# One unread 128-column product per pass of the gate and up loops, and no drain before them

## The reference, cut to what matters

```python
def swiglu(h, w_gate, w_up, w_down):
    return (jax.nn.silu(h @ w_gate) * (h @ w_up)) @ w_down
```

## Time and profile before

| | |
|---|---|
| median of 3 executions | 1468.01 us (1467.56 to 1468.77) |
| profiled execution: its time, its span | 1475.34 us, 1473.5 us |
| PE busy | 1450.0 us, 98% of the span |
| DVE busy | 1000.9 us, 68% |
| ACT busy | 808.7 us, 55% |
| mean granted share of TensorE's clock | 0.996 |
| first loop (layer `f0`), second loop (layer `f1`) | from 82.48 us to 253.95 us, from 600.25 us to 778.43 us |

### The profile page before, as it was taken

One profiled execution on the slowest core, in us unless ns is written; L12 is line 12 of the kernel. 1 busy time (PEld: TensorE's weight loads), 2 busy tenths in 40 slices (PEclk: granted clock), 3 DMA queues, 4 the chain that ended last, 5 costly groups with the idle time before them and its releaser, 6 DMA issues.

```text
span 1473.5 us, 23721 instructions
## 1 busy us (share of the span) xinstructions
PE 1450.0 (98%) x8739; PEld 1260.8 (86%) x8739; DVE 1000.9 (68%) x1447; ACT 808.7 (55%) x1240; POOL 128.4 (9%) x77
## 2 busy tenths in 40 slices
PE   9999999999999999999999999999999899999997
PEld 9999999888986789999998888888678788888875
DVE  7499998433684345888984336335784799898885
ACT  6456666222555434566663325443882478887774
POOL 0520000000000005200000000000110012222111
PEclk9999999999999999999999999999999999999999
DMA  6223333322320213223333232322007499999994
GB/s 258 87 86 114 103 100 113 133 93 101 115 86 1 72 61 112 72 99 114 114 105 124 86 117 70 132 86 86 30 1 285 181 357 395 392 392 393 382 374 121
DMA packets 36216, 226.28 MB, mean 154 GB/s; under 512 B 5271, under 2 KB 5527, under 8 KB 11824
## 3 DMA queue, kind: packets, MB, share of 16 engines
q1 hardware_dynamic: 31248, 211.53, 38.3%
q0 software_dynamic: 4608, 13.22, 3.9%
q10 hardware_dynamic: 288, 0.55, 0.1%
HBM read 215.22 MB, written 13.63 MB: 155 GB/s over the span
## 4 chain that ended last, share of the span: by engine, by line
PE 55%; DMA 5%; DVE 2%; ACT 2%; issue 1%; POOLq 0%; ACTq 0%; DVEq 0%; SPq 0%
PE PS L275 16%; PE PS L277 16%; PE PS L276 16%; DMA eraw<-experts 4%; PE PS L2089 1%; PE PS L2109 1%; PE PS L2100 1%; PE PS L2851 1%; PE PS L1863 0%; DVE WEL L2985 0%; PE PS L2487 0%; ACT WEH L2922 0%; PE PS L316 0%; DMA out<-X,expert_index 0%; PE PS L2874 0%
## 5 line engine op out<-in xcount | busy, mean ns | idle before, releaser
L270 DVE TENSOR_TENSOR WL<-raw,WH 128x2048 fp32r<-128x2048 f32 x53 | 124.5, 2349 | 217.3 <-ACT WH L265 217.2
L2985 DVE TENSOR_TENSOR WEL<-eraw,WEH 128x2048 fp32r<-128x2048 f32 x96 | 217.6, 2286 | 21.2 <-ACT WEH L2922 20.9
L265 ACT ACTIVATE WH<-raw 128x2048 fp32r<-128x2048 f32 x51 | 97.7, 1916 | 221.4 <-PE PS L277 221.4
L2922 ACT ACTIVATE WEH<-eraw 128x2048 fp32r<-128x2048 f32 x96 | 182.2, 1914 | 33.9 <-DMA eraw<-experts 23.4
L275 PE MATMUL PS<-AH,WL 128*128 128x256 f32 (+1 forms) x624 | 181.5, 291 | 2.1 <-DVE WL L270 0.9
L276 PE MATMUL PS<-AL,WH 128*128 128x256 f32 (+1 forms) x624 | 180.7, 290 | 0.0
L277 PE MATMUL PS<-AH,WH 128*128 128x256 f32 (+1 forms) x624 | 180.7, 290 | 0.0
L275 PE MATMUL PS<-WH,AL 128*128 128x512 f32 (+2 forms) x416 | 155.0, 372 | 0.6 <-DVE AL L2321 0.3
L277 PE MATMUL PS<-WH,AH 128*128 128x512 f32 (+2 forms) x416 | 152.5, 367 | 0.0
L276 PE MATMUL PS<-WL,AH 128*128 128x512 f32 (+2 forms) x416 | 152.5, 367 | 0.0
L275 PEld LDWEIGHTS PS<-AH,WL 128*128 128x128 f32 x624 | 118.1, 189 | 5.8 <-DVE WL L270 1.3
(11 more groups left out here) (395 smaller groups left out, 3503.5 us busy)
## 6 DMA issues: line engine op xcount, KB each, us to landing
eraw<-experts SPq DMA_DIRECT2D x96, 1024.0 KB, 16.1
raw<-stream SPq DMA_DIRECT2D x94, 1024.0 KB, 4.9
out<-X SPq DMA_DIRECT2D x5, 512.0 KB, 7.0
moe_rows<-moe_rows_g SPq DMA_DIRECT2D x5, 512.0 KB, 6.5
X<-x SPq DMA_DIRECT2D x4, 512.0 KB, 6.0
ffn_row<-rows SPq DMA_DIRECT2D x2, 512.0 KB, 10.3
final_row<-rows SPq DMA_DIRECT2D x2, 512.0 KB, 6.9
cst<-consts SPq DMA_DIRECT2D x1, 739.5 KB, 15.3
```

Of the source, the lines that this page charges most:

```text
L265: act.activation(unit_home(WH, u, at), raw[:, u % SLOTS, :], ACT.Copy).then_inc(unit_hi, 1)
L270: dve.tensor_tensor(unit_home(WL, u, at), raw[:, u % SLOTS, :], unit_home(WH, u, at).bitcast(F32), ALU.subtract).then_inc(unit_lo, 1)
L2922: act.activation(WEH[:, k % ESLOTS, :], eraw[:, k % ERAW, :], ACT.Copy).then_inc(unit_hi, 1)
L2985: dve.tensor_tensor(WEL[:, k % ESLOTS, :], eraw[:, k % ERAW, :], WEH[:, k % ESLOTS, :].bitcast(F32), ALU.subtract).then_inc(unit_lo, 1)
```

## The change

Each pass of the loop gets one product of 128 columns. It multiplies a block of the low part of the tokens by itself and writes columns 256 to 384 of bank 7, which nothing reads. It stands ahead of the even unit, behind the two waits of its first quarter. The wait of line 797 is taken out.

```diff
+                def shake(bank, n):
+                    for _ in range(n):
+                        pe.matmul(PS[:, bank, 256:384], AL[:, 3, 0:P], AL[:, 3, 0:P], start=True, stop=True)
+
...
                 pe.wait_ge(silu_made, 4)
-                pe.wait_ge(unit_used, u0 + 4)
                 with nc.Fori(PLAIN, n, engines=(mybir.EngineType.PE,), hint_back_edge=True) as i:
                     for odd in range(2):
                         s = 2 * i - 2 * PLAIN + odd
                         pe.wait_ge(c_made, 4 * s + 4)
                         pe.wait_ge(q_lo, 7 * s + 1)
+                        if not odd:
+                            shake(7, 1)
                         quarter_product(0, s, odd, 0, True, True)
```

## The result

| | before | changed |
|---|---|---|
| median | 1467.78 us | 1477.32 us |
| lowest to highest, executions | 1466.93 to 1468.77, 4 | 1476.07 to 1477.79, 4 |

The ratio is 1.0055 with a 95% interval of 1.0036 to 1.0074. The change costs 9.5 us; 1462.6 had been forecast, and a range that ended at 1471.

A forecast was written before the change was run, and what follows sets the result against it. TensorE was taken to bound both loops, by number of matmuls times distance between starts. Median 1468.0 + 0.6 (drain out -1.7, products +2.3) - 6.0 (eight passes turned fast) = 1462.6 us; range 1461 to 1471.

The forecast's parts named there:

- What bounds the loops: Both loops: TensorE never idle mid-loop; length is matmuls times start distance, 113.3 ns in the first, 117.8 in the second.
- case 1: First loop stays fast, second turns fast in its first pass or so; eight passes gain 6.0 us: 1462.6, chance 0.42.
- the turn at 563.50: Layer f1, behind turning products: slow steps of 118 ns went over to 113.3 ns after five steps, read as slow-to-fast.
- Case 4: Both loops: the product leaves the slow rhythm every time; first loop loses 6.7 us: 1475.3, chance 0.18.
- case 3: Both loops: each product draws the pace anew like a coin; nine of 18 passes slow gives 1468.6 us, chance 0.12.
- The base that failed: Whole kernel: differences worked against the profiled execution of 1475.34 us were applied to the median, 7.3 us lower, 1468.0.
- case 2: Both loops: pace stays, or was not slow unprofiled; only +0.6 us is left: 1468.6, at most 1471, chance 0.28.
- The fixed part: Both loops, apart from pace: drain out -1.7 us, 18 products +2.3, together +0.6, bounds +0.3 to +3.0.
- The first unit's slack: First loop, quarter 4: weights ready 1.11 us before the matmul; starting 0.87 us earlier brings back no wait.

The follow-up runs named there:

- the third trace of before: The kernel before, unchanged, traced once more for one of its shorter executions: 1469.20 us, both loops fast at 172.2 us.
- the first experiments: Four kernels run together: kernel before unchanged 1469.95 us; no drain, no product 1479.58; product, drain kept 1477.99; two products a pass 1472.11.

## Why the prediction was wrong

**What bounds the loops** was right: matmuls times the distance of their starts, with two paces of 113.3 and 117.8 ns, 0.75 us a pass. In every later trace each unit of each loop runs at one of these two on average, apart from a few steps behind an interruption and the one unit of the kernel without drain in which the pace changed.

**The step that failed** is the one of case 1, that the fast rhythm holds through its interruptions, read from one place in the earlier trace rows. A single unread product turns fast into slow in all eight places where the changed kernel puts one behind a fast pass, and slow into fast in all eight others. With the kernels of the experiments there are 82 places inside the loops with one such product, and the rhythm turns over in each. So I had half of it, slow to fast, and none of the other half. A turn by eight products of another type was taken as the likeness of a single one, and the two-product runs show how much the number matters.

Even for the eight the turn at 563.50 was no recovery. At this place of layer `f1` the pace changes over in all 14 traces of this case, in ten from slow to fast and in four from fast to slow (no drain and no product; product with the drain; three products; 192 columns). The first of the four, in the timeline of PE:

```profile
558.99 0.28 PE L276 MATMUL PS<-AL,WH 128*128 128x256 f32 x1
...
561.50 0.28 PE L277 MATMUL PS<-AH,WH 128*128 128x256 f32 x1
561.62 1.04 PE L316 MATMUL PS<-cst,ffn_rows_g 128*128 128x128 f32 x8
...
562.61 0.28 PE L276 MATMUL PS<-AL,WH 128*128 128x256 f32 x1
...
576.51 0.28 PE L277 MATMUL PS<-AH,WH 128*128 128x256 f32 x1
```

The 22 steps ahead are 114.1 ns each (the first three slow, the others 113.3), the 118 behind are 117.8. The two such places between the gate and up products of layer `f0`, one at 41.10 and one 3.6 us behind it that the prediction doesn't count, keep the pace in all 14 traces, fast in eleven and slow in three. The one trace of before could show only one half of this.

Case 4 (slow every time) was wrong too; the truth, a strict alternation with a slow first pass, lay nearest to case 3's nine slow of 18, with ten and no draw.

**The base that failed** is the second step: differences read against a trace with a slow loop were applied to a median with none. I named this in case 2 and gave the whole case 0.28, but case 1, 3 and 4 all kept the slow loop in their sums. Against a usual execution there was nothing to win, and case 3's sum for nine slow passes would have been 1475.3 in place of 1468.6.

**The fixed part** held. A fast loop without drain is 171.4 us for 1512 steps; the changed kernel's is 176.2. Five slow passes are 3.7 of this, nine products at 0.12 are 1.0 and the few slow steps behind each turn 0.1. In both loops that is 7.5 for the pace and 2.3 for the products, as forecast (2.3); the drain gives back 1.7 to 1.8, as forecast (1.7). The sum is +8.0 us, and the traces give 8.1 (span 1475.3 against 1467.2 in the third trace of before). The medians are 9.5 apart by the first four executions of before and 8.4 by the 27 beside the first experiments; the median of the kernel before was 1467.8, 1468.9 and 1469.8 in three sets of executions, so 1 to 2 us of such a difference are open.

**The first unit's slack** was right: in the changed kernel quarter 4 starts at 87.25 and its weights are ready at 86.84, so 0.41 of the 1.11 us of the earlier trace rows is left and nothing waits.

**What stays open** is why a product turns the rhythm. One of 128 columns turns it either way, two keep it either way, three and one of 192 columns keep a fast one (they never met a slow one), one of 256 turned a fast one slow once and never a slow one fast. Eight turning products turn it either way at one place and keep it either way at two others. Neither parity nor the length of the weight load explains all of it. Other operands or another bank for the product were not tried, though the turning products show that a turn does not need these. Why the drain's start is fast in most executions and not in all is open as well.

## What to carry to other kernels

Read the distance between starts and not the busy share: a loop that is 100% busy in two traces can still differ by 4% in pace. Before arguing from one trace, hold its time against the timed executions; here 6.7 of the 7.3 us between them were one slow loop, and the trace to argue from was another one. An interruption put in to shake a loop out of a bad rhythm shakes it out of a good one too, so set the rhythm once, ahead of the loop, by something that leaves it the same in every execution.

## What the runs showed of the hardware

- A stream of fp32r matmuls of 256 columns, each with a weight load, has two steady paces at a granted clock of 1.00, 113.3 and 117.8 ns. It keeps one for 1512 matmuls and across loop returns.
- One 128-column matmul put into this stream turned the pace over in all 82 places, two kept it in all 34, by the traces.
- The pace behind a drained queue differs between executions: 17 of 61 executions of one program had the times of one slow loop. Straight out of the 512-column matmuls ahead of them the loops started slow (both in the trace without drain); with two 128-column products between, fast, in all of 11 and of 10 executions by their times. It is no rule for 512 columns: the run of 256-column matmuls at 35.63 us of the trace before, behind three of 512 columns (line 284), settled at 113.3 ns, and so did its like in 11 of the 14 traces.
- The Trainium skill ("TensorE: Matmul & The Clock Gate", section "Back-to-back issue gap") gives 262 cycles for a matmul of 256 columns by itself, an estimated 109 ns at 2.4 GHz. It has no figure for a stream with weight loads at this width; at 512 columns it gives 131 ns for such a stream. The traces show 113.3 or 117.8 ns at 256 columns and 0.23 us at 512, and the measurement decides.
